# Rounded products for the later half of four embedding-gate tiles

## The reference

```
for i in range(DEPTH_2):
    ...
    h = h + mix
    h = h + hier_moe(rmsnorm_2(h, norm_ffn[i]), ...)
    gate = jax.nn.sigmoid(rmsnorm_2(h, norm_ple[i]) @ w_ple_gate[i] + b_ple_gate[i])
    h = h + gate * (p[i] @ w_ple[i])
return rmsnorm_2(h, norm_final)
```

## Time and profile before

| | |
|---|---|
| median of 3 runs | 1612.22 us (1610.81 to 1614.25) |
| span of the profiled execution | 1606.7 us, from its first to its last instruction |
| median of the runs less this span | 5.5 us |
| PE busy | 1312.8 us, 82% of the span, 9392 instructions |
| DVE busy | 598.5 us, 37% |
| ACT busy | 435.9 us, 27% |
| POOL busy | 213.8 us, 13%, 119 instructions |
| mean granted clock of TensorE | 0.900 |
| transfers | 528.42 MB, mean 329 GB/s |

### The profile page before, as it was taken

One profiled execution on the slowest core, in us unless ns is written; L12 is line 12 of the kernel. 1 busy time (PEld: TensorE's weight loads), 2 busy tenths in 40 slices (PEclk: granted clock), 3 DMA queues, 4 the chain that ended last, 5 costly groups with the idle time before them and its releaser, 6 DMA issues.

```text
span 1606.7 us, 21602 instructions
## 1 busy us (share of the span) xinstructions
PE 1312.8 (82%) x9392; PEld 856.4 (53%) x9392; DVE 598.5 (37%) x1159; ACT 435.9 (27%) x645; POOL 213.8 (13%) x119
## 2 busy tenths in 40 slices
PE   7999999999999987766657758999886775675677
PEld 3787798999999832212212215998521221221226
DVE  4788547885387201001101104785210110110116
ACT  4564455444454210000000003683200000000005
POOL 0224244886400100000000000000000000000000
PEclk9999999999999998777877879999988777877889
DMA  9425543444648999999999999459899999999992
GB/s 400 172 89 230 211 174 144 172 177 145 241 154 344 374 425 428 427 427 427 426 429 427 425 422 382 173 213 381 359 427 425 426 429 426 428 427 427 427 409 106
DMA packets 52624, 528.42 MB, mean 329 GB/s; under 512 B 4784, under 2 KB 4912, under 8 KB 20144
## 3 DMA queue, kind: packets, MB, share of 16 engines
q1 hardware_dynamic: 51952, 525.22, 79.8%
q10 hardware_dynamic: 576, 1.79, 0.3%
HBM read 525.94 MB, written 1.05 MB: 328 GB/s over the span
## 4 chain that ended last, share of the span: by engine, by line
PE 52%; DMA 38%; SPq 3%; DVE 2%; ACT 2%; issue 1%; POOL 0%; DVEq 0%; ACTq 0%
PE bank L672 25%; PE bank L1294 9%; DMA ring<-in_w_up 8%; DMA ring<-in_w_down 7%; DMA work<-in_w_gate 7%; DMA ring<-in_w_gate 6%; DMA work<-in_w_up 4%; DMA work<-in_w_down 4%; PE bank L1314 3%; SPq L566 3%; PE bank L1376 3%; PE bank L665 2%; DMA ring<-in_dense 2%; PE bank L1444 2%; PE bank L914 1%; PE bank L786 1%
## 5 line engine op out<-in xcount | busy, mean ns | idle before, releaser
L1294 PE MATMUL bank<-ring,work 128*32 128x512 f32 x1232 | 319.0, 730 | 135.3 <-DMA ring<-in_w_up 69.8
L672 PE MATMUL bank<-work_rounded,ring_rounded 128*128 128x256 f32 (+1 forms) x2000 | 301.8, 286 | 2.2 <-DVE work_rounded L2099 1.3
L672 PEld LDWEIGHTS bank<-work_rounded,ring_rounded 128*128 128x128 f32 x2000 | 265.9, 188 | 9.4 <-issue 2.9
L672 PE MATMUL bank<-xn_rounded,ring_rounded 128*128 128x256 f32 (+1 forms) x1472 | 248.9, 285 | 1.2 <-DVE xn_rounded L2140 1.2
L1294 PEld LDWEIGHTS bank<-ring,work 128*32 128x32 f32 x1232 | 69.8, 130 | 308.6 <-issue 114.9
L2725 DVE TENSOR_TENSOR work<-work,bank 128x512 f32<-128x512 f32 x16 | 11.0, 688 | 547.0 <-PE bank L1294 547.0
L672 PEld LDWEIGHTS bank<-xn_rounded,ring_rounded 128*128 128x128 f32 x1472 | 202.6, 188 | 5.4 <-issue 2.7
L1294 PE MATMUL bank<-work 128*32 128x512 f32 x496 | 157.6, 677 | 34.5 <-DMA work<-in_w_gate 19.1
L1988 POOL TENSOR_TENSOR ring_rounded<-ring,ring_rounded 128x2048 fp32r<-128x2048 f32 (+1 forms) x35 | 149.2, 4279 | 158.9 <-ACT ring_rounded L1517 158.9
L1517 ACT ACTIVATE ring_rounded<-ring 128x2048 fp32r<-128x2048 f32 (+1 forms) x76 | 133.1, 1797 | 47.2 <-PE bank L672 28.5
L1314 PE MATMUL bank<-ring,work 128*32 128x512 f32 x576 | 123.0, 650 | 16.7 <-DMA ring<-in_w_down 16.7
(11 more groups left out here) (351 smaller groups left out, 1685.3 us busy)
## 6 DMA issues: line engine op xcount, KB each, us to landing
ring<-in_dense SPq DMA_DIRECT2D x47, 2048.0 KB, 8.4
ring<-in_w_up SPq DMA_DIRECT2D x38, 2048.0 KB, 30.2
ring<-in_w_gate SPq DMA_DIRECT2D x36, 2048.0 KB, 29.5
ring<-in_w_down SPq DMA_DIRECT2D x34, 2048.0 KB, 29.3
work<-in_w_gate SPq DMA_DIRECT2D x16, 2048.0 KB, 23.1
work<-in_w_down SPq DMA_DIRECT2D x16, 2048.0 KB, 32.2
spare<-in_w_gate SPq DMA_DIRECT2D x8, 2048.0 KB, 29.0
work<-in_w_up SPq DMA_DIRECT2D x8, 2048.0 KB, 31.9
```

The lines of the kernel that those rows point to most:

```text
L672: last = mm(out, rv(high_store[r][:, at:at + P]), rv(x[part][k]), start=opens and k == 0 and j == 0, stop=closes and k == n_k - 1 and j == 2)
L1294: ins = mm(out[slots(y), :], xg[:, k, slots(y)], expert_columns(w, at, 512), start=k == 0, stop=k == KT - 1)
```

## The change

For the first chunk of both layers the products of k = 4 to 7 become rounded ones: `split_step` takes the place of `plain` there. What follows from it:

- The first chunk joins `SPLITS`, with only its later half to be split, in two quarters of 128 x 1024 (`split_parts`): columns 2048 to 3072 hold k = 4 and 5, columns 3072 to 4096 k = 6 and 7. The rounded copies go into a part of `work` (`LATER_HIGH`), the remainders in place.
- ACT makes these copies at the start of `ple`, before the squares; its scaling of k = 4 to 7 into `emb_x` goes.
- POOL makes the two remainders, since the chunk is not in DVE's list `by_dve`.
- PE waits for `xn_ready` of k = 4 to 7 and for `w_low` before k = 4 and before k = 6; it takes the input that DVE makes already for the second chunk.

The core of the diff:

```
+LATER_HIGH = RING + 1
...
+    later_half = halved[1:]
+    whole = (first["w_in_b"],)
...
+            if n in later_half:
+                high_slot[n], high_after[n] = LATER_HIGH, None
+                splits.append(n)
+            elif name in SPLIT and n not in whole:
...
+    high_store = [r[:] for r in ring] + [flat(12288, CHUNK)]
...
+    def split_parts(n):
+
+        return ((CHUNK // 2, 3 * CHUNK // 4), (3 * CHUNK // 4, CHUNK)) if n in LATER_HALF else parts_of(n)
...
-            if k in (0, n_k // 2):
-                name, value = LOW_DONE[chunk, 0 if k == 0 else 1]
+            steps_of = (KT // 2, 3 * KT // 4) if chunk in LATER_HALF else (0, n_k // 2)
+            if k in steps_of:
+                name, value = LOW_DONE[chunk, steps_of.index(k)]
                 pe.wait_ge(S[name], value)
...
+        def split_step(n, use, k, x, ready):
+
+            split_arrived(n, k)
+            pe.wait_ge(S[ready[0]], ready[1] + k)
+            for b in range(2):
+                for i in range(2):
+                    last = split_product(bank[(use + b) % BANKS][:, SEQ * i:SEQ * i + SEQ], n, 2 * b + i, x, k, closes=i == 1)
+                if k == KT - 1:
+                    assert signal(last, "dense_full") == use + b + 1
...
-            plain(n, use, 0, emb_x)
+            plain(n, use, 0, emb_x, len(early))
             scatter(QUADS - 1, (2, 3))
-            for k in range(1, KT):
-                plain(n, use, k, emb_x)
+            for k in early[1:]:
+                plain(n, use, k, emb_x, len(early))
+            ready, x_parts = next_input(), [[x[:, k] for k in range(KT)] for x in (ple_xh, xnT)]
+            for k in late:
+                split_step(n, use, k, x_parts, ready)
             sums()
...
         def ple(layer):
-            embedding_inputs(layer, range(4, KT))
+            split_next()
+            act.wait_ge(S["scat_add"], (layer + 1) * 4 * QUADS)
             for i in range(4):
...
-                for i, (a, b) in enumerate(parts_of(n)):
+                for i, (a, b) in enumerate(split_parts(n)):
...
-            split_low((1 + 3, 1)[layer])
+            split_low((2 + 3, 2)[layer])
```

More of the change, by code:

```diff
@@ L178, in plan @@
     halved = tuple(first[name] for name in ("w_in", "ple0", "ple1"))
-    whole = (*halved[1:], first["w_in_b"])
+    later_half = halved[1:]
+    whole = (first["w_in_b"],)
     loads, until, turn = [0] * (RING + 1), {}, 0
@@ L209, in plan @@
             until[r] = free[n]
-            if name in SPLIT and n not in whole:
-                r = LOAD_SLOTS + len(splits) % 2
+            if n in later_half:
+                high_slot[n], high_after[n] = LATER_HIGH, None
+                splits.append(n)
+            elif name in SPLIT and n not in whole:
+                r = LOAD_SLOTS + len([m for m in splits if m not in later_half]) % 2
                 high_slot[n], high_after[n] = r, held_until.get((n, r), until.get(r))
@@ L226, in plan @@
             low_done[n, half] = (name, made[name])
-    return first, use, free, slot, arrival, load_after, splits, high_slot, high_after, low_done, halved
+    return first, use, free, slot, arrival, load_after, splits, high_slot, high_after, low_done, halved, later_half
 def highs_before(n):
     return 2 * sum(m < n for m in SPLITS)
-FIRST, USE, FREE, SLOT, ARRIVAL, LOAD_AFTER, SPLITS, HIGH_SLOT, HIGH_AFTER, LOW_DONE, HALVED = plan()
+FIRST, USE, FREE, SLOT, ARRIVAL, LOAD_AFTER, SPLITS, HIGH_SLOT, HIGH_AFTER, LOW_DONE, HALVED, LATER_HALF = plan()
 def gate_use(i):
@@ L436, in build @@
     in_a_high, rstd_sq = flat(6144, 2048).rearrange("p (k t) -> p k t", k=KT), bank[5][:, 0:SEQ]
-    high_store = [r[:] for r in ring]
+    high_store = [r[:] for r in ring] + [flat(12288, CHUNK)]
     uu = yg = flat(2048, 2048).rearrange("p (k t) -> p k t", k=KT)
@@ L1367, in moe, with plain @@
             return scatter
-        def plain(n, use, k, x):
+        def plain(n, use, k, x, ks=KT):
             w = arrived(pe, n, 2 * k // KT)
@@ L1379, in plain @@
                     assert signal(last, "dense_full") == use + b + 1
-            if k == KT - 1:
-                plain.done += KT
+            if k == ks - 1:
+                plain.done += ks
+        def split_step(n, use, k, x, ready):
[6 more added lines that the diff above has]
+                    assert signal(last, "dense_full") == use + b + 1
         plain.done = 0
@@ L1396, in ple @@
                 released(pe, use + b - BANKS)
-            plain(n, use, 0, emb_x)
+            plain(n, use, 0, emb_x, len(early))
             scatter(QUADS - 1, (2, 3))
-            for k in range(1, KT):
-                plain(n, use, k, emb_x)
+            for k in early[1:]:
[3 more added lines that the diff above has]
+                split_step(n, use, k, x_parts, ready)
             sums()
-            ready = next_input()
             for b in range(2, 4 + layer):
-                dense_split(use + b, [(n + 1, j % 4) for j in range(*gate_tiles(layer, b))],
-                            [[x[:, k] for k in range(KT)] for x in (ple_xh, xnT)], None if b > 2 else ready)
+                dense_split(use + b, [(n + 1, j % 4) for j in range(*gate_tiles(layer, b))], x_parts, None if b > 2 else ready)
         moe.last_use = [USE["out_a"] + 3, USE["out_b"] + 3]
@@ L1511, in split_half @@
             count["halves"] = count.get("halves", 0) + 1
-            w = arrived(act, n, half)
+            w = arrived(act, n, 1 if n in LATER_HALF else half)
             if HIGH_AFTER[n]:
@@ L1515, in split_half @@
                 act.wait_ge(S[sem], value)
-            a, b = parts_of(n)[half]
+            a, b = split_parts(n)[half]
             signal(act.activation(rv(high_store[HIGH_SLOT[n]][:, a:b]), w[:, a:b], ACT.Copy), "w_high")
```

## The result

| | before | after |
|---|---|---|
| median | 1611.53 us (16 runs, 1607.72 to 1615.68) | 1617.78 us (16 runs, 1613.75 to 1623.56) |
| ratio | | 1.0040, 95% interval 1.0028 to 1.0051 |
| the profiled execution's span | 1606.7 us | 1620.4 us (its time: 1622.17 us) |

The change makes the kernel slower by 6.2 us, by the interval 4.5 to 8.2. The forecast was 1619.0 us. The two spans differ by more, 13.7 us, but 8.3 of that lies ahead of layer 0's first plain product, where nothing has changed (994.91 us here, 986.62 in the earlier trace rows): two single executions differ so by themselves. The change's cost is read from the stages. I call **the stage** what lies between the start of the first chunk's first plain product and the end of the second chunk's 96 rounded products.

The account below looks back on a forecast made before the run. PE alone was taken to bound the gate stages; DVE's lateness behind POOL, net of PE's saving, adds 5.3 us and one clock fall 1.5, +6.8 on 1612.2: 1619.0 us, range 1613.5 to 1622.5.

Parts of the forecast that it names:

- DVE's delay: DVE's run of 16 input steps, held back by POOL's two subtractions: 4.39 us late in layer 0, 4.41 in layer 1.
- the sum: Both layers' later ends on PE: +2.54 and +0.06 us in layer 0, +2.59 and +0.06 in layer 1, together +5.3.
- PE's saving, 1.26 us per layer: First chunk, k = 4 to 7: 16 plain products of 6.91 us become 48 rounded ones of 5.65, if PE never waits.
- Landing, copies, POOL's step: Second weight half lands at 988.9 and 1571.9; ACT copies quarters in 1.0 and 0.95 us; POOL subtracts each in 2.40.
- POOL ahead, one DVE step, POOL again, then DVE's run: Order at DVE's input run: POOL's first quarter from 990.07 to 992.47, one DVE step, second quarter for 2.40 us, remaining DVE steps.
- PE's wait 3.8 us: Before k = 4 in layer 0: its input is ready at 998.51, so PE waits 3.8 us, then works 5.65 us.
- +0.06 for the second chunk: Second chunk's remainders on DVE end at 1006.49, where PE wants their second half at 1006.43: +0.06 us; layer 1 the same.
- One fall of the clock: TensorE's granted clock falls after one of PE's two waits, costing 1.5 us; the forecast case, chance 0.34.
- the sum with no fall: Rival: the wait is cut in two or the clock holds, only +5.3 us, 1617.5 us; chance 0.18.
- The rival with two falls: Both layers' waits cost the clock, 3.0 us on top of 5.3: 1620.5 us; chance 0.28.
- DVE and POOL do not meet: Rival at DVE's input run: it passes by POOL's subtractions, only PE's saving of 2.5 us remains, 1609.7 us; chance 0.11.
- One layer escapes: Rival: a transfer lands at another time than in this execution, +2.6 - 1.3 = +1.3 us, 1613.5 us; chance 0.09.

Follow-up runs that it names:

- experiment 1: Changed kernel with POOL subtracting 8 columns of each quarter instead of 1024, rounded copies replacing remainders in the third product: 1608.96 us against 1610.48 before.
- experiment 3: Changed kernel with DVE's 16 input steps reordered, k = 4 to 7 first, then k = 0 to 3: 1615.07 us against 1610.48 before.
- the second profile: The changed kernel measured and profiled once more, without edit, beside other kernels on the same chip: 1619.78 us against 1611.24 before.
- experiment 8: Changed kernel with only k = 6 and 7 rounded, k = 4 and 5 plain, POOL's first step cut to 8 columns: 1611.52 us against 1611.24 before.
- experiment 4: Changed kernel with DVE's inputs of k = 4 to 7 first, then the first chunk's remainders on DVE instead of POOL: 1611.81 us against 1610.48 before.
- experiment 6: Changed kernel with 7 unused plain products of 128x256 on PE before its wait for k = 4: 1614.39 us against 1611.24 before.

## Why the prediction was right

It named the mechanism and the sign, and its +6.8 us stands against +6.2 measured. DVE's delay was counted 0.60 us too long in each layer, and two terms that the sum had at nothing, 0.15 and 0.19 us, took back more than half of that; so the closeness is in part luck.

1. *PE's saving, 1.26 us per layer.* Confirmed: 1.25 and 1.21 with POOL's work taken away.
2. *Landing, copies, POOL's step.* ACT began its copies 2.27 us from the first plain product in both layers (forecast 2.28 and 2.29), with 1.0 us each; POOL's steps took 2.37 and 2.40 us (forecast 2.40 from the line between two sizes).
3. *POOL ahead, one DVE step, POOL again, then DVE's run.* So it went, in both layers. **DVE's delay was mis-sized**: forecast 4.39 us, measured 3.79 (4.41 less 0.62). The sum let a held step begin anew when POOL ends; the rows show it closing 0.14 us behind POOL. A row that said so was there: the held pair of the earlier trace rows, of the same operation and size as in this run, took 1.05 us and ended at 1118.77, so that its first step, a pitch of 0.27 us earlier, closed 0.14 us behind POOL. The forecast had gone by the other row, an addition of two operands and 512 columns, which ended 0.6 us behind. The order, POOL's second step ahead of DVE's run, came out, but its row did not show it: POOL's subtraction at 428.05 started 0.31 us before the end of the DVE step that it is said to have waited for, and the earlier trace rows has ACT's copy as its releaser. The Trainium skill's page "SBUF — State Buffer", section "SBUF: two separate sides", has the loser of the port pair block fully; the trace agrees, to the end of each POOL instruction.
4. *PE's wait 3.8 us, the layer +2.60 (2.54 and 0.06).* 3.36 and +2.33 at full clock, 0.27 us less per layer. From the 0.60 us of step 3 two terms go off that the sum had at nothing. PE began k = 4 0.15 us behind the end of its input (1006.36 against 1005.74 + 0.47), and the 48 products took 5.84 us behind the wait, where they took 5.65 when PE ran on (experiment 1). The forecast's +0.06 for the second chunk looked like a trifle and wasn't one: it says that DVE's remainders, too, are late by as much as PE, which experiment 3 brought into the open. Putting the cost on the wait at k = 4 was half of the truth; it is the length of DVE's run.
5. *One fall of the clock, 1.5 us.* One, in layer 1, at 1.54 us (31.04 - 29.50). The forecast of 6.8 us against the 6.2 measured is thus nearly all from steps 3 and 4. That it was one of the two waits was luck: the earlier trace rows has one wait with a fall behind it, and no row says how often a wait brings one. The time alone doesn't tell the number of falls either: its interval, 4.5 to 8.2 us, holds the sum with no fall (5.3) as well as that with one; the profile does. The falls are not the same from run to run: the first measurement is 1.6 us above the 4.7 of DVE's delay, about one fall, the second 3.8, two falls and 0.7 us that its interval (6.9 to 12.6 us) covers. The rival with two falls (1620.5 us) was the case in the second profile. The Trainium skill's page "TensorE: Matmul & The Clock Gate", Part 1, has activity release the throttled state; filled waits without a fall agree, and the one unfilled wait that kept its clock shows that standing still did not bring the fall each time.
6. *The rivals.* "DVE and POOL do not meet" fell by the first pair of each layer. "One layer escapes" was not seen in the change's two profiles; its condition, weights that come earlier against DVE's run, is what layer 1 of experiment 8 shows for one POOL step.

What stays open: what separates the wait in layer 0 of the first profile, with its clock kept, from the three that lost it. No run takes that apart.

## What to carry to other kernels

Work moved to an engine that stands idle is not free where its instructions hold up the busy one: here POOL's 4.73 us cost DVE 3.79, and DVE did the same work in 2.36 (experiment 4). Before a wait is charged to the step that shows it, follow the late engine's run to its last consumer: reordering moved the wait from k = 4 to the second chunk and changed the stage by nothing, while shortening DVE's run (its last remainders 15.9 us from the first plain product in place of 19.3) turned the change into a gain. Where TensorE has to wait ahead of a long run of products, unused products in the gap can keep the clock that the wait would cost, as they did in both layers of experiment 6.

## What the runs showed of the hardware that was not expected

- A DVE step held by a POOL instruction closes 0.14 or 0.15 us behind it (the steps of 2.05 and 2.44 us after), where the same step unheld takes 0.35 us.
- POOL can also come in between two steps of a DVE run that is already going: in experiment 8 it began at 991.92, and DVE's next step, at 991.99, took 2.58 us in place of 0.48.
- Equal waits of 3.36 us in one execution were followed once by a full clock and once by a stretch at the lower of its two levels, 1.2 GHz, which cost 1.56 us (7.40 - 5.84).
